# One core, a two-layer trunk: the first projection split by channels, and the modulation chunks placed elsewhere

## The reference, cut to what matters

```
sh1, sc1, g1, sh2, sc2, g2 = adaln(c, ada_w[l], ada_b[l])   # silu(c) @ (1024 x 6144) + bias
h = rmsnorm(x, norm_mix[l]) * (1 + sc1) + sh1
p = h @ w_in                                                # 1024 x 2080
q_lat, kv_lat, k_rope, na_qkv = split(p, [384, 512, 544])
q  = rmsnorm((rmsnorm(q_lat) @ w_q_up), q_gain)             # 8 heads of 96
kv = rmsnorm(kv_lat) @ w_kv_up                              # keys and values, 8 heads
nq, nk = rmsnorm(na_q), rmsnorm(na_k);  nv = na_v           # 8 heads of 64
out = concat(attention(q, k, v), neighbourhood_attention(nq, nk, nv)) @ w_out
x = x + g1 * out
x = x + g2 * experts(rmsnorm(x) * (1 + sc2) + sh2)
```

## Time and profile before

| | us |
|---|---|
| median of three runs | 1270.1 (1269.69 to 1272.78) |
| the profiled execution, its own time | 1273.05 |
| span in the profile | 1271.3 |
| PE busy | 1136.3 (89% of the span) |
| DVE busy | 565.7 |
| ACT busy | 264.4 |
| POOL busy | 172.9 |

### The profile page before, as it was taken

The page is one execution under the profiler, slowest core; times in us unless marked ns, Lnnn a source line. Parts: engine busy times, 40 slices in busy tenths (PEclk is TensorE's granted clock), DMA queues, the critical chain, the costliest instruction groups (busy, mean ns, idle before and its releaser), DMA issues.

```text
span 1271.3 us, 26256 instructions
## 1 busy us (share of the span) xinstructions
PE 1136.3 (89%) x9215; PEld 656.1 (52%) x9216; DVE 565.7 (45%) x1225; ACT 264.4 (21%) x644; POOL 172.9 (14%) x261
## 2 busy tenths in 40 slices
PE   4899968889978889999699999999998788999995
PEld 3554546654664445455365654343556544555553
DVE  0122444463353334444543334778655344444445
ACT  1111324441111112121232112212001211212121
POOL 1044210000011111211100001111000211121210
PEclk9799989999879999999989999899998899999998
DMA  9832499782496899999923222000028599996894
GB/s 319 308 111 85 158 344 387 253 299 91 169 377 255 355 422 378 423 422 410 374 84 122 77 70 96 1 0 1 1 90 340 233 420 421 418 378 271 329 423 171
DMA packets 82734, 314.19 MB, mean 247 GB/s; under 512 B 11160, under 2 KB 12097, under 8 KB 57321
## 3 DMA queue, kind: packets, MB, share of 16 engines
q1 hardware_dynamic: 77098, 298.66, 60.1%
q10 hardware_dynamic: 3616, 7.67, 1.6%
q0 software_dynamic: 1952, 6.90, 1.4%
HBM read 307.82 MB, written 5.39 MB: 246 GB/s over the span
## 4 chain that ended last, share of the span: by engine, by line
PE 81%; DMA 6%; DVE 5%; issue 4%; SPq 2%; ACT 2%; POOLq 0%; POOL 0%; ACTq 0%; DVEq 0%
PE banks L457 77%; DMA arena<-in_ada_b 3%; DVE arena L999 3%; DMA arena<-token_rows,arena 2%; PE banks L717 1%; SPq L1888 1%; PE banks L629 1%; DVE arena L1145 1%; DMA mod_rows<-arena 1%; SPq L1886 1%; ACT arena L1607 1%; ACT arena L1597 1%; PE banks L840 0%; PE banks L508 0%; ACT arena L1514 0%
## 5 line engine op out<-in xcount | busy, mean ns | idle before, releaser
L457 PE MATMUL banks<-arena 32*128 32x256 f32 (+12 forms) x8788 | 1082.3, 418 | 93.4 <-issue 36.7
L457 PEld LDWEIGHTS banks<-arena 128*32 128x32 f32 (+5 forms) x8788 | 604.0, 154 | 546.2 <-issue 405.4
L999 DVE TENSOR_TENSOR arena<-banks,arena 128x64 f32<-128x64 f32 (+3 forms) x282 | 113.3, 413 | 64.0 <-PE banks L457 58.1
L999 DVE TENSOR_TENSOR arena<-arena 128x384 f32<-128x384 f32 (+13 forms) x229 | 133.7, 590 | 4.4
L1264 DVE SCALAR_TENSOR_TENSOR arena<-arena 128x768 f32<-128x768 f32 x81 | 84.3, 1040 | 108.1 <-issue 105.8
L1641 ACT ACTIVATE arena<-banks 128x512 f32<-128x512 f32 x79 | 47.2, 597 | 231.2 <-PE banks L457 231.2
L1800 POOL TENSOR_TENSOR arena<-arena 128x256 f32<-128x256 f32 x81 | 59.1, 729 | 235.9 <-PE banks L457 235.9
L1274 DVE TENSOR_SCALAR arena<-arena 128x64 f32<-128x64 f32 x79 | 15.4, 195 | 163.9 <-ACT arena L1645 163.9
L1779 POOL TENSOR_SCALAR arena<-arena 128x8 f32<-128x8 f32 (+2 forms) x28 | 7.1, 254 | 368.0 <-ACT arena L1498 264.6
L1809 POOL COPY arena<-arena 128x256 f32 x79 | 31.4, 398 | 187.2 <-PE banks L457 158.1
L1364 DVE TENSOR_SCALAR arena<-arena 128x385 f32<-128x385 f32 x24 | 11.6, 481 | 82.4 <-ACT arena L1702 82.4
(11 more groups left out here) (150 smaller groups left out, 454.4 us busy)
## 6 DMA issues: line engine op xcount, KB each, us to landing
arena<-in_moe_w_gate SPq DMA_DIRECT2D x64, 1024.0 KB, 8.2
arena<-in_moe_w_up SPq DMA_DIRECT2D x64, 1024.0 KB, 10.5
arena<-in_moe_w_down SPq DMA_DIRECT2D x64, 1024.0 KB, 10.5
arena<-in_ada_w SPq DMA_DIRECT2D x24, 2048.0 KB
arena<-in_hy_w_in SPq DMA_DIRECT2D x6, 2048.0 KB
arena<-in_attn_w_in SPq DMA_DIRECT2D x3, 2048.0 KB
arena<-mod_rows SPq DMA_DIRECT2D x8, 512.0 KB, 9.5
arena<-in_attn_w_out SPq DMA_DIRECT2D x2, 2048.0 KB
```

The costliest lines, as they stand in the source:

```text
L457: return pe.matmul(out, lhsT, rhs, start=start, stop=stop, skip_group_check=True)
L999: return dve.tensor_tensor(o, p, q, op)
```

## The change

The first projection runs over channels 0 to 511 first (`half(kind, t, 0)`), which needs only modulation chunks 0 and 2, and over channels 512 to 1023 later (`half(kind, t, 1)`). The three `kvr` results share one bank, cleared by DVE ahead of time, and are closed last. Chunks 1 and 3 get two places of their own outside the ring, in memory that is not yet in use. The order of loads becomes: table and x (now on SP's queue, before anything else), chunk 0, chunk 2, win 0, chunk 1, chunk 3, win 1, `chunks[0]`, the bias table, win 2, `chunks[1]`, win 3, `chunks[2]`, up, `chunks[3]`, `chunks[4]`, and so on; the table of places is written out. Four chunks (`chunks[0]` to `chunks[3]`) are multiplied among the nq, nk and nv projections, seven (4 to 10) in units 4 to 10, and nine (11 to 19) among the head pairs. ACT issues the six small gain loads after its first evictions, and POOL issues the cache loads after the fourth chunk. Two warming products stand before the first projection.

The core of the diff (signal bookkeeping left out):

```diff
         def place_of(n):
 
-            return n % 3 if n < 9 else (n - 9) % 2 if n < 15 else (n + 2) % 3
+            return places[n]
 
         def ring(n):
-            return RING + place_of(n) * MSLOT
+            return (RING, RING + MSLOT, RING + 2 * MSLOT, WORK + 2048, MODO)[place_of(n)]
...
-        turn_of = {c: i for i, c in enumerate([(0, n) for n in range(4)] + chunks)}
-        items0 = ([("ada", 0, n) for n in range(4)] + [("win", i) for i in range(4)] + [("up",)]
-                  + [("ada", l, n) for l, n in chunks]
-                  + [("out", 0), ("out", 1)])
+        first_chunks = [(0, 0), (0, 2), (0, 1), (0, 3)]
+        turn_of = {c: i for i, c in enumerate(first_chunks + chunks)}
+        ch = [("ada", l, n) for l, n in chunks]
+        early = ([(("ada", 0, 0), 0), (("ada", 0, 2), 1), (("win", 0), 2), (("ada", 0, 1), 3), (("ada", 0, 3), 4), (("win", 1), 0)]
+                 + [(ch[0], 1), (("win", 2), 2), (ch[1], 1), (("win", 3), 0), (ch[2], 1), (("up",), 2), (ch[3], 1), (ch[4], 1)]
+                 + [(c, i % 2) for i, c in enumerate(ch[5:11])]
+                 + [(c, (2 + i) % 3) for i, c in enumerate(ch[11:20] + [("out", 0), ("out", 1)])])
+        items0 = [k for k, _ in early]
...
-        at_unit = {6 + n: c for n, c in enumerate(chunks[:7])}
-        at_pair = {int(1.9 * n) + 1: c for n, c in enumerate(chunks[7:])}
+        at_unit = {1: chunks[1], 3: chunks[2]}
+        at_unit.update({4 + n: chunks[4 + n] for n in range(7)})
+        at_pair = {int(2.5 * n) + 1: c for n, c in enumerate(chunks[11:])}
...
             def attention():
 
-                n0 = arrived(("win", 0))
-                w = item(n0, KC, WIN0)
+                w = item(arrived(("win", 0)), KC, WIN0)
+
+                def half(kind, t, j):
+                    c0, c1 = (0, QR) if kind == "qlat" else (QR, WIN0)
+                    o = ps[:, place[kind, t], :]
+                    o = o[:, 0:QR] if kind == "qlat" else o[:, t * (WIN0 - QR):(t + 1) * (WIN0 - QR)]
+                    for k in range(4 * j, 4 * j + 4):
+                        last = mm(o, hT[:, k, t * P:(t + 1) * P], w[:, k, c0:c1], kind == "qlat" and k == 0, k == KC - 1)
+                    if j:
+                        close(last, kind, t)
+
                 for t in range(T):
-                    hT_ready(0, t)
-                    for kind, c0, c1 in (("qlat", 0, QR), ("kvr", QR, WIN0)):
-                        o = open_(pe, kind, t, [("lat", t)], 2 * t + (kind == "kvr"))
-                        for k in range(KC):
-                            last = mm(o[:, 0:c1 - c0], hT[:, k, t * P:(t + 1) * P], w[:, k, c0:c1], k == 0, k == KC - 1)
-                        close(last, kind, t)
+                    open_(pe, "qlat", t, [("lat", t)], 2 * t)
+                    name, i = evicted(0, t, 0)
+                    sig(name).at(pe, i)
+                    half("qlat", t, 0)
+                open_(pe, "kvr", 0, [("lat", t) for t in range(T)], 7)
+                place["kvr", 1] = place["kvr", 2] = 7
+                sig("kv_zero").at(pe, 0)
+                ada(0, 1, 6)
+                turn_row(0, 1)
+                half("kvr", 0, 0)
+                ada(0, 3, 6)
+                half("kvr", 1, 0)
+                turn_row(0, 3)
+                half("kvr", 2, 0)
+                for t in range(T):
+                    name, i = evicted(0, t, 1)
+                    sig(name).at(pe, i)
+                    half("qlat", t, 1)
+                    half("kvr", t, 1)
...
                 produce(*units[0])
                 produce(*units[1])
+                ada(*chunks[0], 7)
                 for n, (kind, t) in enumerate(units):
                     if n + 2 < len(units):
                         if units[n + 2] == ("q", 0):
                             for tt in range(T):
                                 produce("nv", tt)
+                                if tt == 1:
+                                    ada(*chunks[3], 7)
...
-            ada(0, 0, 1)
             scaled_transposes(0)
-            for n in range(1, 4):
-                ada(0, n, (n + 1) % 2)
-                turn_row(0, n - 1)
-            turn_row(0, 3)
+            for n in (0, 2):
+                ada(0, n, 6)
+                turn_row(0, n)
+            keep_busy(2, 6)
...
-            ada_row((0, 0))
+            sig("gains").at(dve, 0)
+            sig("kv_zero").by(dve.memset(ps[:, 7, 0:T * (WIN0 - QR)], 0.0), 0)
             for t in range(T):
                 scaled(0, t)
-            sig("gains").at(dve, 0)
-            for n in range(1, 4):
-                ada_row((0, n))
-                columns(0, n - 1)
-            columns(0, 3)
-            for t in range(T):
-                modulated(0, t)
+            for j in range(2):
+                for n in (j, 2 + j):
+                    ada_row((0, n))
+                    columns(0, n)
+                modulated(0, 1, j)
...
+            def first_hT_out(j):
+                sig("colT").at(act, 1 + 2 * j)
+                for t in (0, 2):
+                    o = read(act, "hT", 2 * t + j)
+                    g = min(t, 1)
+                    for k in range(4 * j, 4 * j + 4):
+                        ins = act.activation(hT[:, k, t * P:(t + 1) * P], o[:, k % 4 * P:(k % 4 + 1) * P], ACT.Identity,
+                                             bias=shift[:, k, g:g + 1], scale=slope[:, k, g:g + 1])
+                    sig("hT").by(ins, 2 * j + t // 2)
...
-            act.dma_start(tab, a["tab"][:, 0:TAB]).then_inc(in_const, 16)
-            act.dma_start(x[:, 0, :], a["x_prompt"].rearrange("b t d -> (b t) d")).then_inc(in_x, 16)
-            act.dma_start(x[:, 1:3, :], a["x_sample"].rearrange("b (t p) d -> p (b t) d", p=P)).then_inc(in_x, 16)
...
+            squares(0)
+            first_hT_out(0)
             if stage >= 1:
                 for dst, nme, n in ((qn, "mla_q_norm", QR), (kvn, "mla_kv_norm", KVR), (nqg, "na_q_gain", NAD),
                                     (nkg, "na_k_gain", NAD), (qg, "mla_q_gain", QK), (kg, "mla_k_gain", QK)):
                     act.dma_start(dst, rows(a[nme], 0, n)).then_inc(in_gains, 16)
-            squares(0)
-            hT_out(0)
+            first_hT_out(1)
...
             rms(0)
             if stage >= 1:
+                sig("psum_ada").at(pool, 3)
                 pool.dma_start(V[:, 3, NAW:], a["cache_na_v"].rearrange("b a t h d -> (b a t) (h d)")).then_inc(in_ctxv, 16)
-                sig("psum_hT").at(pool, 5)
...
+            sp.dma_start(tab, a["tab"][:, 0:TAB]).then_inc(in_const, 16)
+            sp.dma_start(x[:, 0, :], a["x_prompt"].rearrange("b t d -> (b t) d")).then_inc(in_x, 16)
+            sp.dma_start(x[:, 1:3, :], a["x_sample"].rearrange("b (t p) d -> p (b t) d", p=P)).then_inc(in_x, 16)
+            groups = {(l, n): (l, j) for l in range(2) for j, n in enumerate((5, 9, 11))}
+            for n, k in enumerate(items0):
                 load(k)
...
+                if k == ch[0]:
+                    sp.dma_start(bias.rearrange("p a b c d -> p (a b c d)"), a["bias"]).then_inc(in_bias, 16)
+                done = items0[max(n - 2, 0)]
+                if done[0] == "ada" and done[1:] in groups:
+                    store_mod(*groups[done[1:]])
+                    if done[1:] == (0, 5):
+                        load_gate(0, 0)
```

More of the change, by code:

```diff
@@ L309, in build @@
             landed[k] = loads[place_of(n)]
-        item_loaded = [sem(f"item_loaded{i}") for i in range(3)]
+        item_loaded = [sem(f"item_loaded{i}") for i in range(5)]
         gu_loaded = [sem(f"gu_loaded{i}") for i in range(4)]
@@ L654, in attention, with keep_busy @@
                     turn_row(1, n)
-            def keep_busy(n):
-                o = open_(pe, "idle", turn[0], [])
+            def keep_busy(n, bank=None):
+                o = open_(pe, "idle", turn[0], [], bank)
                 for _ in range(n):
@@ L1007, in ada_row @@
                     if n < 4:
[L1008 removed]
+                        sig("psum_colT").at(dve, turned_row(l, n))
                     else:
@@ L1038, in scaled, with modulated @@
                 sig("xdiag").by(dve.tensor_scalar(xdiag[:, t, :], ident, rstd[:, t:t + 1], None, ALU.mult), u // 2 * 3 + t)
[L1040 to L1042 removed]
+            def modulated(u, t, j=1):
+                sig("colT").at(dve, u // 2 * 4 + 1 + 2 * j)
+                o = read(dve, "hT", (u * 3 + t) * 2 + j)
                 g = min(t, 1)
[L1044 to L1045 removed]
+                for k in range(4 * j, 4 * j + 4):
+                    ins = dve.tensor_scalar(hT[:, k, t * P:(t + 1) * P], o[:, k % 4 * P:(k % 4 + 1) * P], slope[:, k, g:g + 1],
                                             shift[:, k, g:g + 1], ALU.mult, ALU.add)
[L1047 removed]
+                name, i = evicted(u, t, j)
+                sig(name).by(ins, i)
             def residual(l):
@@ L1081, in attention @@
                 mean_squares(0)
+                ada_row(chunks[0])
```

(25 more changed lines are left out.)

52 lines of the change are left out of this document (28 added, 24 removed).

## The result

| | before | changed |
|---|---|---|
| median of the runs | 1269.89 us (4 runs) | 1252.18 us (4 runs, 1246.98 to 1256.28) |
| the profiled execution, its own time | 1273.05 | 1246.98 |
| span in the profile | 1271.3 | 1245.2 |

What follows compares the result with a forecast made beforehand. PE was taken to bound the kernel, waiting for transfers before and after a stretch with mostly idle DMA engines. Terms -8.4 + 9.2 - 9.7 - 10.1 = -19.0 us gave 1251 us against the median of 1270.1, range 1243 to 1264.

Steps and rivals of the forecast that it cites:

- Part 1: First projection in halves between the chunks: it ends at 61 us and not 69.4, 8.4 us less.
- Part 2: Four chunks among the nq, nk and nv projections, each 2.31 us with nothing hiding them: 9.2 us more.
- Part 3: Seven chunks in the units with loads issued earlier, fewer waits on modulation loads: 9.7 us less.
- the 1 us that was to be a sign of being right: Units: no wait on a modulation load over 1 us would show the prediction right.
- Part 4: Heads: nine chunks in place of thirteen, 1.6 us each, plus a wait and some half clock gone: 10.1 us less.
- The ring: Units: rival that loads in the two slots take 11.84 us and not 8.8, losing 8 us: 1259; chance 0.15.
- The better loads: First stage: rival that loads run better than their lag, chunk 3 landing near 39 us: 1245; chance 0.12.
- The clock rival: First projection: rival that bursts between loads bring half clock there and into the next projections, 1294 us; chance 0.07.

Runs made afterwards that it cites:

- Moving the copy: Changed kernel with the last unit chunk moved from unit 10 to 11, in its own bank, its row copied by DVE after the last norm; 1252.0 us, 0.984.
- warming PE: Changed kernel with seven more warming products, four in the wait for chunk 3, three in the wait for unit 11's norm; 1260.0 us, 0.987.
- without the stall: Kernel before with the first gate's load moved behind all items on SP's queue; 1269.8 us, 0.998 of the kernel before.
- doubling: Changed kernel with the main products of each of the nine chunks among the heads issued twice; 1266.1 us.
- old places: Changed kernel's first projection in halves, but the other twenty chunks where they were before: seven in units 6 to 12, thirteen among head pairs; 1263.2 us, 0.991.
- light side: Changed kernel with the nine chunks among the heads cut to one of eight channel groups, loads and waits kept; 1232.8 us.
- the whole first projection: Changed kernel with all four first chunks multiplied before the first projection again, loads and queues as changed; 1264.7 us, 0.993 of the kernel before.
- old places, late gate: Split kernel with the twenty chunks in their old places and the first gate's load moved behind all items on SP's queue; 1263.5 us.

## Why the prediction was right, point by point

- **Part 1**, -8.4 forecast, -11.0 and -8.5 measured. The curve of bytes put chunk 3 at 43.2 us; PE began it at 41.8 and 42.7. Two terms were off. I gave chunk 3 the 3.83 us of the earlier trace rows, a chunk mostly at half clock (0.58 from 38.9 to 42.7 us there); it ran at a granted clock of 1.00 in one execution of the changed kernel and, with its small half, at 0.68 in the other. And the x loads at SP's head, "worth nothing by itself", are worth 3 to 6 us: with x at its old time PE and not the loads sets the end.
- **Part 2**, +9.2 forecast, +9.7 measured (63.5 to 73.2), in every kernel with the four chunks. No wait in it.
- **Part 3**, -9.7 forecast, -5.9 and -5.2 measured. This is the term that was mis-sized. The new waits on loads were 2.7 and 3.4 us, against 2.5 written; the longest were 1.4 and 1.3, above the 1 us that was to be a sign of being right. What I left out stands at the end of the units: with the last chunk in unit 10, PE has two transposes left and DVE two norms, the first with a rotation. PE stood 2.7 us for it and then ran mostly at half clock (3.66 us in place of 2.2, granted clock 0.56). I had 0.5 for ACT. Moving the copy or warming PE did not give it back; in both, PE still waited for DVE's norms (2.8 and 1.5 us). The source of the gain was partly misread too: the 11.84 us after the SP stall was worth 1 to 3 us. That the rest came from giving each chunk a projection to hide its load, and from loads that were issued earlier, is argued from the waits that stayed without the stall; no run separates the two.
- **Part 4**, -10.1 forecast, -13.4 measured. A chunk came to 1.9 us where I took 1.6 (doubling, and old places: 11.9 us less 2.4 of wait and 2 of clock, over four), and to 1.6 from the light side. The lower bound of 0.4 set pairs from the two ends of the heads against each other; like with like in the kernel before, a transpose at 234.89 us stands between the two of the earlier trace rows and gives 5.21 us with a chunk and 3.47 without, 1.7 for the chunk. Half clock among the heads was gone altogether in both profiled executions, worth 3 us by the 0.97 of the earlier trace rows, where I had taken 1.5. That part is luck as far as the runs show: the same chunks and pairs ran at 0.96 in three other kernels, and with their 89.3 us part 4 would have given 10.2.
- **The sum.** The stages gave -20.6 and -17.5 us against -19.0, and the median 17.7. The number came out well in part because part 3, short by about 4 us, and part 4, over by 3.3, offset one another. The span of the first profiled execution was 26.1 us shorter, 5.3 of it behind the heads, where nothing had changed.
- **The rivals.** The ring did not starve: no wait in the units over 1.4 us. The better loads came in half, chunk 3 at 41.8 and not 39. The clock rival, which rests on the low clock of the earlier trace rows and on the 4.99 us that PE had stood for the third chunk, fell, and with the opposite sign: against the whole first projection the split removed the wait of 7.7 us and shortened that of 3.5, both followed by half clock there (chunks 1 and 3 at 4.1 and 4.2 us, granted clock 0.53 and 0.50), and the mean clock up to the end of the first projection rose from 0.90 before to 1.00 and 0.97. So between these kernels the waits that are left tell more than the number of pieces that the projection is cut into. The 384 GB/s of the earlier trace rows, with which part 3 counts, was not the most that the loads reached: in the mean the units moved 306 GB/s, but from 42 to 50 us it was 403:

```profile
42.00:50.00 8.00, 7.29 (x98) 5.59 (x91) 1.99 (x7) 2.90 (x8) 2.44 (x4) 1.00 1.06 403
```

## What to carry to other kernels

When PE waits for loads at both ends of a stretch in which the DMA engines are mostly idle (a share of 0.28 in the projections of the kernel before), split the first consumer so that its first half needs only the first loads, and spread the rest so that each load has a product of its own beside it. Here both together were worth 20.8 and 17.5 us up to the end of the heads; what seems to have counted is the PE work beside each load, not the number of loads. Cost the end of a pipelined stage by itself: when its main product runs out, an engine that was covered all along can set the pace, as DVE did here with a wait of 2.7 us. And compare stages by their events, since here the part that had not changed took between 972 and 985 us.

## What the runs showed of the hardware

The same nine chunks among the same 24 pairs took 86.1 us at a mean granted clock of 1.00 (two executions), 87.3 and 87.7 at 0.98, and 89.2 or 89.3 at 0.96 (three). The instructions were the same but for chunk 10's place and the warming. How long PE had just waited did not say whether half clock would follow: after 2.47 us the next chunk ran at 1.00, after 2.15 us in another kernel at 0.62. In the two kernels with the lowest clock among the heads, 0.91 (light chunks) and 0.92 (whole ones, old places, late gate), 14 us of half clock lay in one piece, from 190 to 204 and from 189 to 203 us, with 1.00 in the 6 us before it and from 205 to 225 us. And in the changed kernel the loads, most of their bytes in transfers of 2 MB, ran at 403 GB/s in the mean from 42 to 50 us.
